# An expert's token list with 112 places in place of 128

## What is computed

```python
D_MODEL, D_FF_EXPERT, N_EXPERTS, TOP_K = 1024, 1792, 8, 2
def swiglu(h, w_gate, w_up, w_down):
    return (jax.nn.silu(h @ w_gate) * (h @ w_up)) @ w_down
def moe_swiglu(h, router, w_gate, w_up, w_down):
    logits = (h @ router).astype(jnp.float32)
    top_v, top_i = lax.top_k(logits, TOP_K)
    wts = jax.nn.softmax(top_v, axis=-1)
    gates = jnp.sum(jax.nn.one_hot(top_i, N_EXPERTS, dtype=jnp.float32) * wts[..., None], axis=-2)
    out = jnp.zeros_like(h)
    for e in range(N_EXPERTS):
        out = out + (gates[..., e:e + 1] * swiglu(h, w_gate[e], w_up[e], w_down[e]).astype(jnp.float32)).astype(h.dtype)
    return out
```

## Time and profile before

| what | value |
|---|---|
| runs of the kernel, median (lowest to highest) | 1411.33 us (1409.72 to 1417.41) |
| span of the profiled execution | 1419.1 us |
| TensorE busy in the span | 1301.8 us, 92% |
| VectorE busy | 941.5 us, 66% |
| ScalarE busy | 707.7 us, 50% |
| moved by DMA | 326.76 MB, mean 230 GB/s |

### The profile page before, as it was taken

One profiled execution on the slowest core, in us unless ns is written; L12 is line 12 of the kernel. 1 busy time (PEld: TensorE's weight loads), 2 busy tenths in 40 slices (PEclk: granted clock), 3 DMA queues, 4 the chain that ended last, 5 costly groups with the idle time before them and its releaser, 6 DMA issues.

```text
span 1419.1 us, 25438 instructions
## 1 busy us (share of the span) xinstructions
PE 1301.8 (92%) x10487; PEld 1126.2 (79%) x10487; DVE 941.5 (66%) x1612; ACT 707.7 (50%) x1188; POOL 10.1 (1%) x22
## 2 busy tenths in 40 slices
PE   4999898987999998998888878999999999999994
PEld 3899756766999997998666657888887979797984
DVE  1675635624555545676358247898899899989986
ACT  2566222214444444563132125776677677767772
POOL 0000000000000000000000000000000000000000
PEclk9999877588999999999776888999999999999997
DMA  9545358553444443456265523898889889979991
GB/s 388 213 154 207 121 183 318 180 215 149 178 179 141 164 186 130 175 202 202 62 226 163 188 110 125 324 358 304 320 336 347 301 324 351 335 281 343 349 339 39
DMA packets 30332, 326.76 MB, mean 230 GB/s; under 512 B 6018, under 2 KB 6530, under 8 KB 8066
## 3 DMA queue, kind: packets, MB, share of 16 engines
q1 hardware_dynamic: 28738, 319.17, 61.3%
q0 software_dynamic: 1472, 5.89, 1.1%
HBM read 319.15 MB, written 5.89 MB: 229 GB/s over the span
## 4 chain that ended last, share of the span: by engine, by line
PE 81%; DVE 9%; DMA 4%; ACT 3%; issue 3%; SPq 0%; DVEq 0%; POOL 0%; ACTq 0%; POOLq 0%
PE bank L747 19%; PE bank L748 18%; PE bank L749 18%; PE bank L1132 4%; DMA ring<-in_w_ada 4%; PE bank L667 3%; PE bank L803 2%; PE bank L1226 2%; PE bank L644 1%; PE bank L699 1%; DVE w_low L2400 1%; DVE win_low L1877 1%; PE bank L1254 1%; PE bank L1005 1%; PE bank L770 1%
## 5 line engine op out<-in xcount | busy, mean ns | idle before, releaser
L2400 DVE TENSOR_TENSOR w_low<-ring,w_high 128x1024 fp32r<-128x1024 f32 x352 | 399.6, 1172 | 46.0 <-ACT w_high L1756 44.5
L1756 ACT ACTIVATE w_high<-ring 128x1024 fp32r<-128x1024 f32 x352 | 342.2, 1016 | 15.1 <-PE bank L749 13.9
L747 PE MATMUL bank<-w_high,hcH 128*128 128x512 f32 x448 | 184.9, 413 | 2.3 <-DVE w_low L2400 1.9
L749 PE MATMUL bank<-w_low,hcH 128*128 128x512 f32 x448 | 176.2, 393 | 0.0
L748 PE MATMUL bank<-w_high,hcL 128*128 128x512 f32 x448 | 176.0, 393 | 0.0
L747 PE MATMUL bank<-w_high,hidH 128*128 128x256 f32 x448 | 128.5, 287 | 3.0 <-DVE w_low L2400 3.0
L749 PE MATMUL bank<-w_low,hidH 128*128 128x256 f32 x448 | 126.7, 283 | 0.0
L748 PE MATMUL bank<-w_high,hidL 128*128 128x256 f32 x448 | 126.7, 283 | 0.0
L747 PE MATMUL bank<-pH,win_high 128*128 128x264 f32 x416 | 119.9, 288 | 2.5 <-issue 2.0
L1388 ACT ACTIVATE arena<-bank 128x264 f32<-128x264 f32 (+8 forms) x128 | 51.7, 407 | 137.7 <-PE bank L644 51.9
L748 PE MATMUL bank<-pH,win_low 128*128 128x264 f32 x416 | 117.9, 283 | 0.0
(11 more groups left out here) (393 smaller groups left out, 2548.5 us busy)
## 6 DMA issues: line engine op xcount, KB each, us to landing
ring<-in_moe_gu SPq DMA_DIRECT2D x56, 2048.0 KB, 8.6
ring<-in_moe_down SPq DMA_DIRECT2D x32, 1792.0 KB, 7.6
ring<-in_w_ada SPq DMA_DIRECT2D x24, 2048.0 KB, 8.9
ring<-in_w_in SPq DMA_DIRECT2D x16, 1536.0 KB, 6.5
ring<-in_ffn_gu SPq DMA_DIRECT2D x11, 2048.0 KB, 7.6
ring<-in_ffn_down SPq DMA_DIRECT2D x8, 1408.0 KB, 5.8
ring<-in_w_out SPq DMA_DIRECT2D x4, 2048.0 KB, 7.7
ring<-in_cache_fox_k SPq DMA_DIRECT2D x32, 128.0 KB, 3.0
```

Source lines behind the costliest of these rows:

```text
L747: mm(out, wh, xh, start=start, stop=False)
L749: return mm(out, wh, xl, start=False, stop=stop)
L1756: A_(split(w_high), src, ACT.Copy).then_inc(sem("w_high_ready"), 1)
L2400: TT(split(w_low), src, split(w_high), ALU.subtract).then_inc(sem("w_low_ready"), 1)
```

## The change

`CAP` becomes 112. Four statements that addressed all 128 partitions of the transposed places and gates now address `CAP`; all other sizes follow from the constant. The moving operand of a gather is 2 x 112 = 224 columns, the standing operand of the gate, up and down matmuls has 112 columns, and the drains of gathered and hidden blocks are 448 and 224 elements long in place of 512 and 256. A list of more than 112 tokens takes a second round.

```diff
-CAP = P
+CAP = 112
 ROUNDS = -(-NT // CAP)
...
                         for g in range(3):
-                            pe.transpose(b[:, g * CH:(g + 1) * CH], G[:, g, j, :].bitcast(F32), C("ident"))
+                            pe.transpose(b[0:CAP, g * CH:(g + 1) * CH], G[:, g, j, :].bitcast(F32), C("ident"))
                         for g in range(3):
-                            ins = mm(b[:, 3 * CH:3 * CH + 1], G[:, g, j, :].bitcast(F32),
+                            ins = mm(b[0:CAP, 3 * CH:3 * CH + 1], G[:, g, j, :].bitcast(F32),
                                      gates[:, g, 2 * q + j:2 * q + j + 1], start=g == 0, stop=g == 2)
...
-                        A_(place_row[:, q % 2, 0, :], bank[6][:, 0:NT], ACT.Copy).then_inc(sem("placed"), 1)
-                        A_(gcol[:, q % 2, 0:1], bank[6][:, 3 * CH:3 * CH + 1], ACT.Copy).then_inc(sem("placed"), 1)
+                        A_(place_row[0:CAP, q % 2, 0, :], bank[6][0:CAP, 0:NT], ACT.Copy).then_inc(sem("placed"), 1)
+                        A_(gcol[0:CAP, q % 2, 0:1], bank[6][0:CAP, 3 * CH:3 * CH + 1], ACT.Copy).then_inc(sem("placed"), 1)
...
-                        CP(place_row[:, q % 2, 1, :], bank[7][:, 0:NT]).then_inc(sem("gated"), 1)
-                        CP(gcol[:, q % 2, 1:2], bank[7][:, 3 * CH:3 * CH + 1]).then_inc(sem("gated"), 1)
+                        CP(place_row[0:CAP, q % 2, 1, :], bank[7][0:CAP, 0:NT]).then_inc(sem("gated"), 1)
+                        CP(gcol[0:CAP, q % 2, 1:2], bank[7][0:CAP, 3 * CH:3 * CH + 1]).then_inc(sem("gated"), 1)
```

## The result

The changed kernel took 1402.72 us (median of nine runs, 1399.76 to 1410.52), the kernel before 1417.35 us beside it: a ratio of 0.992 with a 95% interval of 0.9893 to 0.9946 (the ratio is taken over all runs; the two medians alone would give 0.990). A second set of runs gave 0.9973 (0.9947 to 0.9999), and the kernel before against itself there 1.0023 (0.9991 to 1.0055). So the change is a gain of about half a per cent, and one such set can't tell 0.3% from 0.8%. The forecast was 1406 us, 0.4% less than the 1411.33 of three runs.

The account below looks back on a forecast made before the run. The prediction took TensorE to bound the experts stage, about 540 us, with VectorE close behind. Terms of 1.0 + 1.8 + 0.5 + 1.2 + 0.7 + 0.5 = 5.7 us off 1411.3 gave 1406 us, range 1394 to 1462.

Parts of the forecast that it names:

- second round: Rival: the whole experts stage, 540 us, repeats when a list exceeds the places, to about 1950 us; chance 0.01.
- down, 112 standing columns: Down matmuls: a standing-operand load 14 ns shorter gains between nothing and 17.5 us; 1 us taken.
- gate and up, 112 standing columns: Gate and up matmuls: the load lies under a stream twice as long, so nothing is gained.
- hidL (and hidH): VectorE's subtraction ahead of a slab's fourth w_low: 32 fewer elements, 33 ns, 56 times, 1.8 us.
- transposes: 112 transposes of the hidden block: moving columns fall from 128 to 112, 0 to 1.5 us; 0.5 taken.
- gathers: 192 gather matmuls: 224 moving columns in place of 256, up to 2.9 us gained; 1.2 taken.
- places turned: 72 records with G standing (transposes and gate columns), at most 14 ns each, 0 to 1.0 us; 0.5 taken.
- drains of the gathers, G: Shorter first-pair hcL drains, 0.3 us, and G 96 elements shorter, four times, 0.4 us: 0.7 together.
- waits of PEld for w_low: Sign in the experts stage: TensorE's load waits for w_low sum to a little under 22.4 us.
- narrow gather: Rival, line 1226: below 256 columns the rounded type falls to plain f32's pace, 49.5 us cost, 1456 us; chance 0.20.
- load rival: Faster rival: the load sets the down pace, up to 13 ns a matmul, 1391 us at best; chance 0.10.
- favoured width: Slower rival: 112-column loads are no longer hidden, down matmuls go from 120 to 190 ns, 1500 us; chance 0.03.

## Why the prediction was right, point by point

The mechanism held: no count of matmuls changed, the stage stayed TensorE's (under way in 535.5 of 541.6 us), nothing that was added waits. The forecast gain of 5.7 us is 7.1 in the stage, 6.7 in the second profiles. The sizes of the terms did not hold, and two of the errors cancelled.

| term | forecast, us | in the stretch, before to after (means of two) | by undoing it |
|---|---|---|---|
| down, 112 standing columns | 1.0 (0 to 17.5) | 166.7 - 163.2 = 3.5 | 166.7 - 162.3 = 4.4 |
| gate and up, 112 standing columns | 0 | with hidL, below | 314.7 - 314.3 = 0.4 |
| hidL (and hidH) | 1.8 | gate and up 315.4 - 314.4 = 1.0 | 1.1 to 1.5 |
| transposes | 0.5 | 7.6 - 7.3 = 0.3 | 0.5 |
| gathers | 1.2 | 17.5 - 16.1 = 1.4 (three pairs) | 17.4 - 16.1 = 1.3 |
| places turned | 0.5 | 5.6 - 5.2 = 0.4 (three pairs) | not undone by itself |
| drains of the gathers, G | 0.7 | no group of their own | none seen |

With 0.2 us more in the scatters these make the 6.4 of the stretch. The 20 us ahead of it are 0.4 shorter in both pairs of profiles; what the first pair's gathers, drains and places gave lies in there, together with the clock. Nothing of the 7 us is left without a place. Over the eight runs without the trouble of the 64 rows and with 112 columns or fewer the down matmuls take 161 to 163 us, and 166.7 in each of the three with 128; gate and up take 315.3 to 315.5 us in the four runs with 256-element drains of the hidden block and 312 to 314.7 in those with shorter ones.

**Mis-sized: the loads of the down matmuls.** This is the largest part, more than half of the stretch's gain. I took 1 us because the load is hidden at half clock, and because 256 and 264 columns had the same pace. The first is true there and says nothing of full clock. The second had another reading: the 256-column matmuls were held at 120 by 128 standing columns, since they run at 117 with fewer. The 264-column ones always had 128 standing columns, and no run shows them with fewer. The experiments with 128, 112, 96 and 64 columns show that it is a small hold with an end: 3.5 to 4.4 us, not the 17.5 of the bound. The starts came 117 ns apart, between the forecast's sign of 118 to 120 and the rival's of 107 to 113.

**Over-sized: hidL, the drains and G.** They were to give 2.5 us. hidL gave 1.0 to 1.5, and the others at most the 0.4 ahead of the stretch. That the sum still came near is luck: the down matmuls gave 2.5 us more than taken, these about 1 less.

**The time** came out 3 us under the forecast, and that is not the change's doing: the two medians lie 14.6 us apart, and the stage shows 7. The forecast was taken off 1411.33, the median of three runs, where nine have 1417.35.

**Gate and up** kept their sum with 112 standing columns, as forecast; their undisturbed starts went from 230 ns apart to 232 or 233, which I had only as 3 us either way for addresses.

**The waits of PEld for w_low** did not shrink. They are counted from the end of the load before, which is 13 ns shorter (175 against 188): over 88 waits that alone would add 1.1 us, and 0.5 were added. The starts of gate and up that lie 280 ns or more behind the one before fell from 111 to 74 (113 to 72 in the second profiles); how much of that is hidL's and how much the slower pace's was not separated.

**The rivals.** The narrow gather did not come: 224 columns took 109 ns from start to start and 192 took 107, where plain f32's pace would be 378 for 224. The load rival came in part, 3.5 to 4.4 us of its 7.8 to 15.6, and ends above 112 columns. (Its 15.6 rest on 1.8 us left in a down stretch; the earlier trace rows leave 22.7 - 20.4 = 2.3, which would have let all 17.5 count.) The favoured width was not lost: loads of 112 columns have records of 175 ns, on the line of 192 for 128 and 135 for 64, and stay hidden. So the Trainium skill's rule in TensorE: Matmul & The Clock Gate, section Weight-path perf modes — Fast Weight Load (FWL) and DoubleRow, that a fast load needs exactly 128 weights and an input that is not FP32, has nothing to take away here; the trace agrees only in that the rounded 32-bit loads run like plain f32 ones, 192 ns beside 190. There was no second round.

**The range** reached to 1462 for the narrow gather. That doubt was real, since the trace of before had no such matmul; it cost the range most of its width.

## What to carry to other kernels

A smaller standing operand is worth what its drains, transposes and the moving sides built from it save, each an eighth here, and a few ns of pace where few columns move past it; under 512 moving columns its width was worth 0.5 us at most. Compare runs by the one stage that a change touches, cut at rows that both traces have, and look at the granted clock in it: here the stage repeats within 0.5 us while the whole time moves by 10 to 18, yet a clock that rose earlier in one run made a cost of 0.5 us look like a gain of 0.9. Cut behind the rise, the same runs repeat within 0.3. Watch what a change of width does to the matmuls that take the result as an operand: with half the rows in use they can lose more than the width gave.

## What the runs showed of the hardware that was not expected

- A 256-column matmul of the rounded type takes 120.0 ns from start to start with 128 standing columns and 117 to 118 with 112, 96 or 64. Yet a gather, which has 128 standing columns too, takes 109 with 224 moving and 107 with 192. So neither the load nor the stream alone needs 120; why the two together do stays open. With 512 columns moving it is the other way round: 230 ns with 128 standing columns, 232 to 233 with 112 or 96.
- Matmuls with 64 standing rows between matmuls with 128 lose the early load at both borders, 10.5 us for 32 groups, 0.33 us each; with 112 or 96 rows that does not happen.
- The rounded type moves 224 and 192 columns without a step in the pace.
- In the same place of programs that differ in a few sizes the clock rose at different times: the first 12 us of the stage had 0.50 to 0.87 of it (0.60 and 0.63 in two executions of one program).
